# A transformer layer on one core: attention exponentials multiplied by their softmax factor before the transposes, outputs kept transposed for the out-projection

## The chip, the core and the metric

The kernel runs as one program on one core of a Trainium2 chip. The metric is the device time of one execution in microseconds. A core has TensorE (PE in the profile, its weight loads PEld), VectorE (DVE), ScalarE (ACT), GpSimd (POOL) and SyncE (SP), which work side by side and meet at semaphores. PE writes to PSUM; the other engines read it and move results to SBUF.

## The reference, cut to what matters

One decoder layer with 1024 tokens of width 1024, all in float32: a feed-forward half step, token mixing, and a second feed-forward half step. The token mixing is what the change touches:

```python
h = u @ w_in                                  # 1976 columns: queries, keys, values, gate logits, latents
# sparse attention, 8 heads in 2 groups of 4, head width 64; e = exp(s - max s) under the mask, l = sum e
o_nsa = g0 * softmax(q k_cmp) v_cmp + g1 * softmax(q k_sel) v_sel + g2 * softmax(q k_win) v_win
#        63 compressed keys           all causal keys (16 of 16 blocks)  window of 512 keys
# g = sigmoid(gate logits), one per token, head and branch
# latent attention, 8 heads, causal
o_mla = softmax((q_nope k_nope + q_rope k_rope) * scale) v
y = concat([o_nsa, o_mla]) @ w_out
x = layer_norm(ALPHA * x + (1 + gate) * y)
```

## The kernel before, in words

Every product keeps float32 precision by splitting each operand into a high part (rounded for PE) and a low part (the rest), and adding two or three products. So every operand of PE costs ACT one pass (`hi`, a copy) and DVE one pass (`lo`, a subtraction).

The kernel goes stage by stage. Those that matter here: `sparse_inputs` (890 to 924 us in the profile), the sparse attention `nsa` (to 1217), the inputs of the latent attention (to 1273), the latent attention `mla` (to 1449), the turning of the heads' outputs `turn3` (to 1462) and the out-projection `out` (to 1555). All outputs of the input projection lie in one SBUF tile `h` (128 tokens x 8 row tiles x 1976 columns), and the attention writes its results over the queries there.

Both attentions run through `attend` on a list of `Unit`s. A unit is four rows of scores (128 x up to 1024 keys) that share keys: in `nsa` one tile of 128 tokens, one group (four heads) and one branch (0 is causal over i+1 key blocks, 1 the window of up to 5 blocks, 2 the compressed keys, one block of 64), 48 units in all; in `mla` one head and one half of the tokens, 16 units of 4 or 8 key blocks. The steps of a unit:

- **stage**: PE turns the queries, ACT and DVE split them (for `mla` also keys);
- **score**: PE computes scores and adds masks, DVE takes the row maximum (`neg_max`), ACT writes `exps` and its row sums;
- **turn**: for each key block four PE transposes of 128 x 128 exponentials into one of three PSUM banks (`ring`), ACT copies `turned_hi`, DVE subtracts `turned_lo`;
- **apply**: PE multiplies values (64 columns of high parts beside 64 of low parts) with `turned_hi` and then with `turned_lo` into `out_ps`; it has 128 rows (high and low results) and 512 columns (four rows of tokens);
- **finish**: ACT copies `out_ps` to `out_sb` (L2769), PE turns it back with four transposes (L2741), DVE adds high and low halves (`joined`, L2816) after computing the factor one over the row sum (L2809, L2813), and POOL multiplies by factor and gate and adds the branches (L2829 to L2842). In `nsa` POOL also scales the latents in 16 of these steps (`scale_latents`, L2915).

The order on each engine is written out by `plan`, which simulates the steps with prices from a table (`pe_price`, `act_price`, `dve_price`) and takes at each moment the step that can start first. Each engine runs its list strictly in that order. `exps` has 3 rooms in `nsa` and 4 in `mla`, so scores run at most that many units ahead of the turns.

After `mla`, `modulated_transpose` ("turn3") turns the 64 blocks of outputs with PE into `u_hi` and `u_lo`, while SP fetches the first four chunks of `w_out` and the rows `x` to which the result is added. Then `project` ("out") runs: DVE multiplies a chunk of weights by a gate row (L2003), ACT and DVE split it (L1983, L2006), and PE makes 24 matmuls of 128x512 for each of 16 chunks (L2044).

## Time and profile before

| | |
|---|---|
| median of three runs | 2229.32 us (2226.71 to 2231.69) |
| profiled execution | 2232.52 us, of which the span of its instructions is 2230.7 us |
| PE, DVE, ACT, POOL busy, share of the span | 95%, 68%, 45%, 27% |
| `nsa`, 924.4 to 1217 us | 292.6 us; PE busy 275.2, DVE 238.0, ACT 226.4, POOL 78.4 |
| `mla`, 1272.7 to 1450 us | 177.3 us; PE 169.2, DVE 129.1, ACT 117.4, POOL 9.8 |
| `turn3`, 1450 to 1464.8 us | 14.8 us; PE 9.4, DVE 11.6, ACT 9.2 |
| `out`, 1464.8 to 1555 us | 90.2 us; PE 89.1, DVE 29.6, ACT 9.5 |

Busy times are unions: where an instruction starts before the last one has ended, the overlap counts once. The mean of a single instruction is therefore a little longer than the distance to the next.

### The profile page before, as it was taken

Reading aid. Unit: us, or ns where it says so; the run is one execution under the profiler, and the core shown is the slowest. Engines: PE = TensorE matmul, PEld = TensorE weight load, DVE = VectorE, ACT = ScalarE, POOL = GpSimd, SP = SyncE. Lnnn points to the kernel's source line nnn. Section 1 sums busy time; section 2 is a strip of 40 time slices with the busy share of each in tenths; the row PEclk is TensorE's granted clock in tenths of the full one; section 3 lists DMA queues with packets and bytes.
Section 4 is the critical chain, followed back from the end, with each engine's and each line's share of the span. In section 5 each row is a group of like instructions: output and inputs, shape, how many; then the busy total and the mean of one; then the engine's idle time right before and its main releaser. Section 6 shows DMA issues by size and latency. Waiting matters only on the chain. (4 is left out here: it accounts for less than half of the span.)

```text
span 2230.7 us, 29121 instructions
## 1 busy us (share of the span) xinstructions
PE 2115.3 (95%) x10361; PEld 1771.7 (79%) x10361; DVE 1508.7 (68%) x2361; ACT 1001.9 (45%) x1925; POOL 599.0 (27%) x597
## 2 busy tenths in 40 slices
PE   5999999999999999799998899998999999999997
PEld 4888888878887887688886789877788888887885
DVE  6877777766886414687887577744765555558689
ACT  3433333334554112887886467621733323324443
POOL 0366656611100000132312000000245555540301
PEclk9999999999998999799999899989999999999998
DMA  7255544468831310300000000041333333347975
GB/s 268 88 168 170 166 165 162 168 206 267 249 109 56 126 46 18 117 1 1 1 1 1 1 1 1 1 151 36 112 118 113 104 118 109 105 127 259 293 258 100
DMA packets 193638, 254.46 MB, mean 114 GB/s; under 512 B 18192, under 2 KB 116560, under 8 KB 193495
## 3 DMA queue, kind: packets, MB, share of 16 engines
q1 hardware_dynamic: 178088, 208.04, 28.1%
q0 software_dynamic: 15408, 44.57, 7.7%
q8 instruction: 83, 1.36, 0.2%
q14 instruction: 59, 0.48, 0.1%
HBM read 212.72 MB, written 43.52 MB: 115 GB/s over the span
## 5 line engine op out<-in xcount | busy, mean ns | idle before, releaser
L781 DVE TENSOR_TENSOR ffn2A_u<-ffn2A_u,ffn_banks 128x512 f32<-128x512 f32 x60 | 41.2, 687 | 118.5 <-PE ffn_banks L725 112.4
L2757 ACT ACTIVATE nsaa_exps<-nsaa_scores,nsaa_neg_max 128x64 f32<-128x64 f32 (+8 forms) x192 | 108.3, 578 | 23.5 <-DVE nsaa_neg_max L2790 15.1
L2805 DVE TENSOR_TENSOR nsaa_turned_lo<-nsaa_ring,nsaa_turned_hi 128x512 fp32r<-128x512 f32 (+1 forms) x148 | 96.7, 683 | 23.4 <-ACT nsaa_turned_hi L2766 22.2
L1315 DVE SCALAR_TENSOR_TENSOR late_part_late<-ada_rows,far_silu_c,late_part_late 128x1024 f32<-128x1024 f32 x56 | 107.2, 1914 | 3.3 <-DMA ada_rows<-in_w_ada 3.2
L602 ACT ACTIVATE ffn1A_t_hi<-ffn1A_t 128x512 fp32r<-128x512 f32 x80 | 48.5, 628 | 132.2 <-POOL ffn1A_t L595 100.3
L602 ACT ACTIVATE ffn2A_t_hi<-ffn2A_t 128x512 fp32r<-128x512 f32 x80 | 48.4, 628 | 122.1 <-POOL ffn2A_t L595 93.8
L2044 PE MATMUL in_acc<-mix_in_w_hi,mix_in_u_hi 128*128 128x494 f32 x256 | 99.4, 388 | 0.7 <-PEq L85 0.7
L2044 PE MATMUL in_acc<-mix_in_w_lo,mix_in_u_hi 128*128 128x494 f32 x256 | 99.1, 387 | 0.0
L2044 PE MATMUL in_acc<-mix_in_w_hi,mix_in_u_lo 128*128 128x494 f32 x256 | 99.0, 387 | 0.0
L725 PE MATMUL ffn_banks<-ffn1S_s_hi,ffn1A_t_hi 128*128 128x512 f32 x240 | 93.8, 391 | 0.0
L725 PE MATMUL ffn_banks<-ffn1S_s_hi,ffn1A_t_lo 128*128 128x512 f32 x240 | 93.4, 389 | 0.0
L725 PE MATMUL ffn_banks<-ffn2S_s_hi,ffn2A_t_hi 128*128 128x512 f32 x240 | 93.4, 389 | 0.0
L725 PE MATMUL ffn_banks<-ffn1S_s_lo,ffn1A_t_hi 128*128 128x512 f32 x240 | 93.4, 389 | 0.0
L725 PE MATMUL ffn_banks<-ffn2S_s_lo,ffn2A_t_hi 128*128 128x512 f32 x240 | 93.4, 389 | 0.0
L725 PE MATMUL ffn_banks<-ffn2S_s_hi,ffn2A_t_lo 128*128 128x512 f32 x240 | 93.4, 389 | 0.0
L2766 ACT ACTIVATE nsaa_turned_hi<-nsaa_ring 128x512 fp32r<-128x512 f32 (+1 forms) x148 | 83.3, 599 | 20.1 <-PE nsaa_ring L2725 19.3
L2725 PE MATMUL nsaa_ring<-all_ident,nsaa_exps 128*128 128x128 f32 (+1 forms) x592 | 82.9, 275 | 2.7 <-DVE nsaa_turned_lo L2805 2.5
L2006 DVE TENSOR_TENSOR mix_in_w_lo<-mix_in_w_raw,mix_in_w_hi 128x494 fp32r<-128x494 f32 x28 | 18.8, 672 | 97.4 <-ACT mix_in_w_hi L1983 97.4
L619 DVE TENSOR_TENSOR ffn2A_t_lo<-ffn2A_t,ffn2A_t_hi 128x512 fp32r<-128x512 f32 x80 | 73.8, 945 | 13.9 <-ACT ffn2A_t_hi L602 12.9
L781 DVE TENSOR_TENSOR ffn1A_u<-ffn1A_u,ffn_banks 128x512 f32<-128x512 f32 x60 | 41.0, 684 | 58.5 <-PE ffn_banks L725 58.5
L2725 PEld LDWEIGHTS nsaa_ring<-all_ident,nsaa_exps 128*128 128x128 f32 (+1 forms) x592 | 68.1, 138 | 11.0 <-DVE nsaa_turned_lo L2805 4.2
L997 PE MATMUL ffn_banks<-ffn2B_d_hi 128*128 128x512 f32 x188 | 73.6, 392 | 2.5 <-ACT ffn2R_p L1040 1.7
(643 smaller groups left out, 6921.2 us busy)
## 6 DMA issues: line engine op xcount, KB each, us to landing
ada_rows<-in_w_ada POOLq DMA_DIRECT2D x56, 512.0 KB, 4.7
ffn_raw_g<-in_ffn_wg SPq DMA_DIRECT2D x44, 512.0 KB, 3.7
ffn_raw_u<-in_ffn_wu SPq DMA_DIRECT2D x44, 512.0 KB, 4.9
early_w<-in_w_ada SPq DMA_DIRECT2D x16, 512.0 KB, 7.0
mix_in_w_raw<-in_w_in SPq DMA_DIRECT2D x32, 247.0 KB, 2.6
ffn_rest<-in_ffn_wd SPq DMA_DIRECT2D x29, 256.0 KB, 5.0
hidden<-ffn1A_c SPq DMA_DIRECT2D x22, 256.0 KB, 4.5
hidden<-ffn1A_u SPq DMA_DIRECT2D x22, 256.0 KB, 5.0
```

Of the source, the lines that this page charges most:

```text
L602: act.activation(self.b_hi[w][:, :], self.block_of(w), ACT.Copy).then_inc(self.rounded, 1)
L619: dve.tensor_tensor(self.b_lo[w][:, :], self.block_of(w), self.b_hi[w][:, :].bitcast(F32), ALU.subtract).then_inc(self.split, 1)
L725: last = pe.matmul(out, b[w][:, cols], u[a][:, c, :], start=(not joins and c == 0 and m == 0), stop=(c == KC - 1 and m == 2), skip_group_c ...
L781: dve.tensor_tensor(out, base, bank, ALU.add).then_inc(self.mixed, 1)
L997: last = pe.matmul(self.banks[:, 4 * QUAD[p] + i, :], h[:, rows], w[:, HALF:D], start=(j == 0 and at == 0 and not JOINS[p]), stop=(j == PA ...
L1315: dve.scalar_tensor_tensor(out=part_late[:, v, :], in0=ada[:, n % 2, :], scalar=silu_c[:, k:k + 1], in1=part_late[:, v, :], op0=ALU.mult, ...
L2006: dve.tensor_tensor(lo[:, k, :], raw[:, k, :], hi[:, k, :].bitcast(F32), ALU.subtract).then_inc(split, 1)
L2044: last = pe.matmul(acc[:, i, 0:width], u[:, c, i * P:(i + 1) * P], w[:, c % slots, :], start=(c == 0 and m == 0), stop=(c == DC - 1 and m ...
L2725: last = pe.transpose(bank[0:u.keys, r * P:(r + 1) * P], exps[n % slots][:, r, k * u.keys:(k + 1) * u.keys], ident[:, :])
L2757: made = act.activation(u.kept(r, exps[n % slots]), u.seen(r, scores[:, m % 2, :]), ACT.Exp, bias=neg_max[:, n % SUMS, r:r + 1], accum_out ...
L2766: act.activation(turned_hi[0:u.keys, j % copies, cols], bank[0:u.keys, cols], ACT.Copy).then_inc(hi_done, 1)
L2805: dve.tensor_tensor(turned_lo[0:u.keys, j % copies, cols], bank[0:u.keys, cols], turned_hi[0:u.keys, j % copies, cols].bitcast(F32), ALU.s ...
```

## The change

1. **Weighing ahead.** The exponentials are multiplied in place by gate / row sum before they are transposed. The first `by_vector` key blocks are done by DVE, four `tensor_scalar` (one for each row) in a step `weigh`; in `nsa` `by_vector` is (blocks + 1) // 3 for branch 0 and zero for the others, in `mla` it is 0 for a first half and 3 for a second. Each other key block is one POOL `tensor_tensor` of 128x4x128 elements (4x64 for the compressed branch, fewer rows at the diagonal in `mla`). A turn waits for its weighing, no longer for the exponentials.
2. **Factor.** A step `factor` on DVE makes max(sum, 1e-30) * (1 + exp(-gate logit)) in one instruction, and its reciprocal. `gates` holds 1 + exp(-logit), made by ACT with Exp and a DVE addition at the end of `sparse_inputs`. DVE also takes over `scale_latents`.
3. **One PSUM group for three branches.** The three branches of a tile are summed in `out_ps`: `out_ps` opens with branch 0 and closes with branch 2 (16 groups in `nsa`, and 16 in `mla`, one for each unit).
4. **Folding in place of finishing.** At the end of a group ACT copies the half of `out_ps` that lies on the other partitions into `other`, and DVE adds it to the half in place and writes the result to `h`, still transposed. The 4 transposes, the copy, `joined` and the POOL work of each unit go.
5. **Compressed branch.** Values lie twice in `vc` (partitions 0 to 63 and 64 to 127), high and low parts of the turned exponentials one above the other, so that its apply is one matmul.
6. **Rooms.** Each branch of `nsa` has two rooms for its exponentials (six in all), some in columns of `h` that are no longer read; `mla` has four as before.
7. **Out-projection.** `turn3` goes. In `project` ACT copies and DVE subtracts 128x1024 elements of `h` for each chunk of its first block (`u_hi`, `u_lo`), and the loads of weights, gate row and `x` are issued there.

```diff
@@ dve_price, pool_price
+    if kind == "weigh":
+        return 4 * (60 + u.by_vector * u.keys * 0.52)
...
+    return 100 + (4 - u.weighed_rows(k)) * u.keys * 2.9
@@ needs (plan)
+        if kind == "factor":
+            return [("act", last_score[n])]
+        if kind == "weigh":
+            return [("dve", ("factor", n, 0))]
@@ attend, tensor
-                    pe.wait_ge(exped, last_score[n] + 1)
+                    if k < u.by_vector:
+                        pe.wait_ge(weighed_dve, weigh_no["weigh", n, 0] + 1)
+                    else:
+                        pe.wait_ge(weighed_pool, weigh_no["weigh", n, k] + 1)
...
-                    if k == 0 and n:
-                        pe.wait_ge(out_moved, n)
...
+                    if k == 0 and u.opens and u.group:
+                        pe.wait_ge(folded, u.group)
+                    start, stop = u.opens and k == 0, u.closes and k == len(u.blocks) - 1
+                    if u.one_block:
+                        last = pe.matmul(out_ps[:, :], u.value_of(0), turned_hi[:, j % copies, :], start=start, stop=stop)
...
-                else:
-                    pe.wait_ge(out_moved, n + 1)
-                    for r in range(4):
-                        last = pe.transpose(bank[:, r * P:(r + 1) * P], out_sb[:, r, :], ident[:, :])
@@ attend, vector
+                elif kind == "factor":
+                    b = n % SUMS
+                    dve.wait_ge(exped, last_score[n] + 1)
...
+                        dve.scalar_tensor_tensor(out=floor[:, b, :], in0=sums[:, b, :], scalar=1e-30, in1=u.gate,
+                                                 op0=ALU.max, op1=ALU.mult).then_inc(floored, 1)
+                    if beside is not None:
+                        beside(dve, n)
+                    dve.wait_ge(floored, n + 1)
                     dve.reciprocal(factor[:, b, :], floor[:, b, :]).then_inc(factored, 1)
...
+                elif kind == "weigh":
+                    dve.wait_ge(factored, n + 1)
+                    for r in range(4):
+                        at = u.room[:, r, 0:min(u.widths[r], u.by_vector * u.keys)]
+                        last = dve.tensor_scalar(at, at, factor[:, n % SUMS, r:r + 1], None, ALU.mult)
+                    last.then_inc(weighed_dve, 1)
+                elif kind == "fold":
+                    dve.wait_ge(moved, u.group + 1)
+                    folding.dve(dve, u.group, out_ps, other).then_inc(folded, 1)
@@ attend, gpsimd
+                pool.wait_ge(factored, n + 1)
+                top = u.weighed_rows(k)
+                at = u.room[:, top:4, k * u.keys:(k + 1) * u.keys]
+                by = factor[:, n % SUMS, top:4].unsqueeze(2).to_broadcast([P, 4 - top, u.keys])
+                pool.tensor_tensor(at, at, by, ALU.mult).then_inc(weighed_pool, 1)
@@ project
+            if reload is not None:
+                chunks.ahead(sp)
             load(0, slots)
+            if reload is not None:
+                for i in range(TT):
+                    sp.dma_start(out[:, i, :], reload[i * P:(i + 1) * P, :]).then_inc(out_in[0], 16)
...
+                if u_raw is not None and n == 0:
+                    act.activation(u_hi[:, c, :].rearrange("p (i q) -> p i q", q=P), u_raw[c], ACT.Copy).then_inc(u_hi_done, 1)
...
+                if u_raw is not None and n == 0:
+                    dve.wait_ge(u_hi_done, c + 1)
+                    dve.tensor_tensor(u_lo[:, c, :].rearrange("p (i q) -> p i q", q=P), u_raw[c],
+                                      u_hi[:, c, :].bitcast(F32).rearrange("p (i q) -> p i q", q=P), ALU.subtract).then_inc(u_split, 1)
```

How the lists change, at three places. First DVE in `nsa`, in the tiles with five or more key blocks, around the factor of a branch-0 unit. Before (`floor`, `factor` and `joined` are the finish):

```order
L2809 TENSOR_SCALAR nsaa_floor<-nsaa_sums 128x4
L2813 RECIPROCAL nsaa_factor<-nsaa_floor 128x4
L2816 TENSOR_REDUCE nsaa_joined<-nsaa_ring 128x256
L2805 TENSOR_TENSOR nsaa_turned_lo<-nsaa_ring,nsaa_turned_hi 128x512
L2786 TENSOR_REDUCE nsaa_neg_max<-nsaa_scores 128x1 x2
```

Now:

```order
L2831 SCALAR_TENSOR_TENSOR nsaa_floor<-nsaa_sums,masks_gates 128x4
L2836 RECIPROCAL nsaa_factor<-nsaa_floor 128x4
L2823 TENSOR_TENSOR nsaa_turned_lo<-nsaa_ring,nsaa_turned_hi 128x512
L2841 TENSOR_SCALAR h_h<-h_h,nsaa_factor 128x256 x4
L2823 TENSOR_TENSOR nsaa_turned_hi<-nsaa_ring,nsaa_turned_hi 64x512
```

Four instructions on the exponentials (here in a room in `h`) stand one subtraction behind the reciprocal, ahead of the next subtractions and maxima.

POOL in `nsa`, its first rows there. Before:

```order
L2829 TENSOR_TENSOR nsaa_factor_g<-nsaa_factor,masks_gates 128x4
L2842 TENSOR_TENSOR h_h<-nsaa_joined,nsaa_factor_g 128x256
L2915 TENSOR_SCALAR h_h<-h_h,sparse_rstd 128x384
L2829 TENSOR_TENSOR nsaa_factor_g<-nsaa_factor,masks_gates 128x4
L2837 TENSOR_TENSOR nsaa_joined<-nsaa_joined,nsaa_factor_g 128x256
L2840 TENSOR_TENSOR h_h<-h_h,nsaa_joined 128x256
```

Now (a branch 0 and a branch 1 run together where the tile's rooms have one name):

```order
L2856 TENSOR_TENSOR nsa_exps<-nsa_exps,nsaa_factor 128x4x128 x5
L2856 TENSOR_TENSOR nsa_exps<-nsa_exps,nsaa_factor 128x256
L2856 TENSOR_TENSOR h_h<-h_h,nsaa_factor 128x4x128 x7
L2856 TENSOR_TENSOR nsa_exps<-nsa_exps,nsaa_factor 128x256
L2856 TENSOR_TENSOR nsa_exps<-nsa_exps,nsaa_factor 128x4x128 x8
```

POOL now has a run of large multiplications for each unit, released by the same reciprocal as DVE's four.

PE from the end of `mla` into the out-projection. Before:

```order
L2735 MATMUL mlaa_out_ps<-mlaa_turned_lo,latent_v 128x128
L2741 MATMUL mlaa_ring<-all_ident,mlaa_out_sb 128x128 x4
L85 UNCONDITIONAL_BRANCH
L203 UNCONDITIONAL_BRANCH
L145 MATMUL turn_tp<-all_ident,h_h 128x128 x64
L85 UNCONDITIONAL_BRANCH
L2035 UNCONDITIONAL_BRANCH
L2044 MATMUL out_acc<-out_w_hi,mix_out_u_hi 128x512
```

Now:

```order
L2757 MATMUL mlaa_out_ps<-mlaa_turned_hi,latent_v 128x128
L2758 MATMUL mlaa_out_ps<-mlaa_turned_lo,latent_v 128x128
L86 UNCONDITIONAL_BRANCH
L2015 UNCONDITIONAL_BRANCH
L2026 MATMUL out_acc<-out_w_hi,mix_out_u_hi 128x512
```

The last 4 transposes of `mla` and the 64 of `turn3` are gone, and the first matmul of the out-projection is the next that PE does.

## Rows read from the trace of the kernel before

**Rows 1.** The page's first part: busy time, share of the span, instructions.
```profile
PE 2115.3 (95%) x10361; PEld 1771.7 (79%) x10361; DVE 1508.7 (68%) x2361; ACT 1001.9 (45%) x1925; POOL 599.0 (27%) x597
```

**Rows 2.** Table by stretch: from:to, us, busy (instructions) per engine, clock, DMA.
```profile
924.40:1217.00 292.60, 275.23 (x1784) 234.91 (x1784) 237.96 (x444) 226.40 (x613) 78.36 (x143) 0.98 0.03 9
...
1272.70:1450.00 177.30, 169.21 (x1066) 150.54 (x1067) 129.10 (x244) 117.35 (x276) 9.81 (x16) 0.97 0.00 1
1450.00:1464.80 14.80, 9.40 (x65) 9.15 (x63) 11.58 (x19) 9.16 (x17) 0.00 (x0) 0.73 0.93 354
1464.80:1555.00 90.20, 89.09 (x384) 73.35 (x384) 29.58 (x48) 9.48 (x15) 0.00 (x0) 0.98 0.13 42
```

**Rows 3.** Groups of instructions in `nsa`: busy us, mean ns, idle before, releaser.
```profile
L2816 DVE TENSOR_REDUCE nsaa_joined<-nsaa_ring 128x256 f32<-128x512 f32 x48 | 32.0, 666 | 5.0 <-PE nsaa_ring L2741 5.0
...
L2741 PE MATMUL nsaa_ring<-all_ident,nsaa_out_sb 128*128 128x128 f32 x192 | 29.3, 275 | 2.6 <-ACT nsaa_out_sb L2769 1.6 <-DVE nsaa_joined L2816 0.5 <-DVE nsa_q L2879 0.4
...
L2837 POOL TENSOR_TENSOR nsaa_joined<-nsaa_joined,nsaa_factor_g 128x256 f32<-128x256 f32 x32 | 19.6, 613 | 14.2 <-DVE nsaa_joined L2816 14.2
...
L2879 DVE SCALAR_TENSOR_TENSOR nsa_q<-nsaa_ring,nsa_q 64x256 fp32r<-64x256 f32 x32 | 13.5, 422 | 6.3 <-ACT nsa_q L2874 5.8
...
L2735 PE MATMUL nsaa_out_ps<-nsaa_turned_lo,sparse_vc 64*128 64x512 f32 x16 | 6.3, 393 | 0.0
```

**Rows 4.** The same view of `mla`.
```profile
L2741 PE MATMUL mlaa_ring<-all_ident,mlaa_out_sb 128*128 128x128 f32 x64 | 9.6, 273 | 0.8 <-ACT mlaa_out_sb L2769 0.8
```

**Rows 5.** Timeline near the end of `mla`: start, us, engine, line.
```profile
1444.66 0.46 PEld L2741 LDWEIGHTS mlaa_ring<-all_ident,mlaa_out_sb 128*128 128x128 f32 x4
...
1445.09 0.19 PEld L2735 LDWEIGHTS mlaa_out_ps<-mlaa_turned_hi,latent_v 128*128 128x128 f32 x1
```

**Rows 6.** Groups on DVE over the whole run.
```profile
L667 DVE CAST ffn1S_a_hi<-plain_u 128x512 fp32r<-128x512 f32 x8 | 3.4, 421 | 1.6 <-ACT plain_u L641 1.6
...
L974 DVE TENSOR_TENSOR ffn2B_d_lo<-ffn_rest,ffn2B_d_hi 128x1024 fp32r<-128x1024 f32 x9 | 11.0, 1219 | 0.0
```

**Rows 7.** Timeline in `nsa`, POOL and DVE side by side.
```profile
991.30 1.25 POOL L2915 TENSOR_SCALAR h_h<-h_h,sparse_rstd 128x384 f32<-128x384 f32 x1
...
992.06 0.51 DVE L2809 TENSOR_SCALAR nsaa_floor<-nsaa_sums 128x4 f32<-128x4 f32 x1
992.60 0.18 DVE L2813 RECIPROCAL nsaa_factor<-nsaa_floor 128x4 f32<-128x4 f32 x1
```

**Rows 8.** The line L2809: durations ns min/median/max, first and last start.
```profile
L2809 DVE TENSOR_SCALAR nsaa_floor<-nsaa_sums x48: 148/160/507, 943.9 to 1214.5; 128x4 f32<-128x4 f32 x48
```

**Rows 9.** Timeline in the second feed-forward stage, POOL and DVE side by side.
```profile
1610.89 1.75 POOL L595 TENSOR_TENSOR ffn2A_t<-ffn_raw_u 128x512 f32<-128x512 f32 x1
...
1611.41 1.78 DVE L671 TENSOR_TENSOR ffn2S_s_lo<-plain_u,ffn2S_s_hi 128x512 fp32r<-128x512 f32 x1
...
1612.72 1.61 POOL L595 TENSOR_TENSOR ffn2A_t<-ffn_raw_g,ffn2A_t 128x512 f32<-128x512 f32 x1
1613.11 1.77 DVE L692 TENSOR_TENSOR plain_u<-plain_u 128x512 f32<-128x512 f32 x1
1614.81 0.68 DVE L671 TENSOR_TENSOR ffn2S_s_lo<-plain_u,ffn2S_s_hi 128x512 fp32r<-128x512 f32 x1
```

**Rows 10.** Timeline of `turn3` and the start of the out-projection.
```profile
1447.82 0.61 POOL L2842 TENSOR_TENSOR h_h<-h_h,mlaa_factor 128x256 f32<-128x256 f32 x1 [0.97 <-DVE h_h L2816]
1449.52 0.34 SPq L1890 DMA_DIRECT2D w_out_gate<-gate_rows  x1
...
1462.65 0.69 DVE L2003 TENSOR_TENSOR w_out_w_raw<-w_out_w_raw,w_out_gate 128x512 f32<-128x512 f32 x1 [0.40 <-PEq L85]
...
1464.78 0.80 PE L2044 MATMUL out_acc<-out_w_hi,mix_out_u_hi 128*128 128x512 f32 x1 [5.40 <-DVE out_w_lo L2006]
```

**Rows 11.** DMA issues: KB each, median us from issue to landing.
```profile
w_out_w_raw<-in_w_out SPq DMA_DIRECT2D x16, 256.0 KB, 2.7
mix_out_x<-x_rows SPq DMA_DIRECT2D x8, 512.0 KB, 9.2
```

More of the change, by code:

```diff
@@ L1892, in ahead, with project @@
             self.load(sp, 0, c)
-def project(nc, stage, chunks, blocks, u_hi, u_lo, out, out_in=None, beside=None):
+def project(nc, stage, chunks, blocks, u_hi, u_lo, out, out_in=None, beside=None, u_raw=None, reload=None):
     slots, width, gated_too = chunks.SLOTS, chunks.width, chunks.gate_dram is not None
@@ L2039, in one @@
                     pe.wait_ge(split, n * DC + c + 1)
+                    if u_raw is not None and n == 0:
+                        pe.wait_ge(u_split, c + 1)
                     for i in range(TT):
@@ L2429, with __init__ @@
 class Unit:
-    def __init__(self, blocks, keys, first_row, key_of, widths, mask_of, value_of, out, adds, gate, before, terms, stage_price):
+    def __init__(self, blocks, keys, first_row, key_of, widths, mask_of, value_of, group, opens, closes, gate, before, terms,
+                 stage_price, by_vector, room):
         self.blocks = blocks
@@ L2439, in __init__ @@
         self.value_of = value_of
-        self.out = out
-        self.adds = adds
+        self.group, self.opens, self.closes = group, opens, closes
         self.gate = gate
@@ L2543, in plan @@
         applying += [("apply", n, k) for k in range(len(u.blocks))]
-        finishing += [("finish", n, 0)]
+        factors += [("factor", n, 0)]
+        for k0, k1 in u.parts_weighed():
+            (by_vector if k0 < u.by_vector else by_pool).append(("weigh", n, k0))
+        if u.closes:
+            folding += [("fold", n, 0)]
     scores = [x for x in scoring if x[0] == "score"]
@@ L2564, in needs @@
                 return [("dve", x)]
+            if kind == "fold":
+                return [("pe", ("apply", n, len(u.blocks) - 1))]
             if kind == "turn" and turn_no[x] >= copies:
@@ L2568, in needs @@
         if engine == "dve":
[L2569 removed]
+            return [("pe" if kind == "score" else "act", x)]
         found = []
[L2571 removed]
+        if kind in ("turn", "stage") and len(ring) >= BANKS:
             found.append(("dve", ring[len(ring) - BANKS]))
@@ L2914, in scale_latents, with halves, act, dve @@
                 at = h[:, i, col:col + rank]
-                pool.tensor_scalar(at, at, rstd[:, which, i:i + 1], None, ALU.mult)
-        tiles = list(range(2, TT)) + [0, 1]
+                dve.tensor_scalar(at, at, rstd[:, which, i:i + 1], None, ALU.mult)
+        class Folding:
+            def halves(self, group, out_ps):
+                rows = out_ps[:, :].rearrange("p (c odd q) -> p c odd q", c=2, odd=2)
+                for odd in range(2):
+                    own, far = slice(odd * HD, (odd + 1) * HD), slice((1 - odd) * HD, (2 - odd) * HD)
+                    yield own, rows[own, :, odd, :], rows[far, :, odd, :]
+            def act(self, act, group, out_ps, other):
+                for own, here, there in self.halves(group, out_ps):
+                    last = act.activation(other[own, 0:2 * P].rearrange("p (c q) -> p c q", c=2), there, ACT.Copy)
+                return last
+            def dve(self, dve, group, out_ps, other):
+                g, i = group // TT, tiles[group % TT]
+                for own, here, there in self.halves(group, out_ps):
+                    at = h[own, i, COL_Q + g * HPG * HD:COL_Q + (g + 1) * HPG * HD].rearrange("p (c q) -> p c q", c=2)
+                    last = dve.tensor_tensor(at, here, other[own, 0:2 * P].rearrange("p (c q) -> p c q", c=2), ALU.add)
+                return last
@@ new lines, in sparse_attention @@
+        tiles = list(range(2, TT)) + [0, 1]
+        vacant = {0: [s.sb("exps0", [P, 4, T]), h[:, 0:4, COL_KC:COL_KC + 6 * P]],
+                  1: [s.sb("exps1", [P, 4, 5 * P]), h[:, 4:8, COL_KC:COL_KC + 5 * P]],
+                  2: [s.sb(f"exps2{m}", [P, 4, CMP_PAD]) for m in range(2)]}
+        rooms = {}
+        for g in range(GROUPS):
+            for i in tiles:
+                for b in range(3):
+                    n = 1 if b == 0 and i >= 6 and vacant[0][0].shape[2] < T else 0
+                    rooms[b, i, g] = vacant[b].pop(n)
+                    vacant[b].append(rooms[b, i, g])
@@ L2976, in unit @@
             b = head % 2
-            col = COL_QM + head * HD
-            out = h[:, 4 * half:4 * half + 4, col:col + HD]
             def key_of(r, c0, w):
```

247 lines of the change are left out of this document (108 added, 139 removed).

## The prediction

> **What bounds the kernel now.** I read the page's totals first [rows 1]: PE is busy 95% of the span, DVE 68%, POOL 27%. A share over the whole run says little about one stage, so next comes the table by stretch [rows 2]. In `nsa` PE works 275.2 of 292.6 us and DVE 238.0, in `mla` 169.2 and 129.1 of 177.3. PE sets both lengths, and DVE is not far behind in `nsa` (81%). `turn3` is 14.8 us, then 5.4 of its last microseconds are a wait of PE [rows 10]. So the change, which takes work from PE, gains only if nothing else comes up to meet it. POOL, at 78.4 us in `nsa`, is to become a large worker there.
>
> **PE's part.** The finish of a unit has four transposes. Their group lists 29.3 us in `nsa` for 48 units, 0.61 us each, and 9.6 us in `mla` for 16 [rows 3, 4]; but matmuls overlap, and the weight loads show that the next work is let in 0.43 us after the first of four (1444.66 to 1445.09) [rows 5]. I take 0.43: 20.6 us in `nsa`, 6.9 in `mla`; the group's own sums are the upper ends. The second apply of the compressed branch goes 16 times: 6.3 us by its row [rows 3] as the upper end, and by overlap, as above, some 4 (taken). PE in `nsa` falls to about 251, in `mla` to 162.
>
> **DVE's part, alone.** In `nsa` 48 `joined` of 0.666 go, 32.0 us [rows 3]. Folding adds 16 times two 64x256 operations. None of this kind is in the trace; the nearest, with a PSUM and an SBUF operand and this shape, took 0.422 [rows 3]: 13.5 us. Weighing adds 14 units (seven tiles in two groups) x 4 instructions of 128, 256 or 384 columns. The nearest SBUF-to-SBUF operation with one tensor in is a cast of 512 columns in 0.421 [rows 6]; with 0.16 for the shortest [rows 8], a column costs about 0.5 ns, so 0.22 to 0.36 us each and 56 x 0.27 = 15 us. The 16 scalings of latents (384 or 256 columns) are 5 us likewise. Sum: 238.0 - 32.0 + 13.5 + 15 + 5 = 240 us. In `mla`: 16 `joined` less (10.7 at the same 0.67), 16 folds of 512 columns (0.68, as a 128x512 operation took in [rows 9]) 10.9, 8 x 4 weighings at 0.36 11.4: 129.1 + 11.6 = 141 us. ACT loses: 48 copies of 512 columns against 32 of 256. It bounds nothing.
>
> **POOL's part.** One multiplication with a broadcast factor took 0.613 for 256 columns [rows 3]; 512 columns should be 1.23. Each group has 54 of these (66 key blocks less 12 of DVE) and 8 small ones: 2 x (54 x 1.23 + 8 x 0.61) = 143 us, half of the stage. As a sum that is no bound. In `mla` it is 8 x 24 row blocks x 0.31 = 59 us.
>
> **What the two do to each other.** This is the term on which the forecast rests. In [rows 7] POOL works from 991.30 to 992.55, and DVE's `floor`, four elements wide and 0.16 as a rule, begins at 992.06 and lasts 0.51: it ends just behind POOL. The longest of 48 is 0.507 at a median of 0.160 [rows 8]. The reciprocal behind it isn't touched (0.18). With work queued on both sides they alternate [rows 9]: POOL from 1610.89 to 1612.64, DVE's operation stands until 1613.19 (1.78 instead of 0.68), POOL's next from 1612.72 to 1614.33, DVE's next again 1.77; once POOL is done, 0.68. So one DVE operation from SBUF to SBUF that meets POOL waits for the rest of one POOL operation, and the next waits for a whole one.
>
> Now DVE's four weighings stand one subtraction (0.68) behind the reciprocal that also releases POOL's run for the same unit. The first waits for half of a POOL operation, 0.6, the others 1.23 each, as long as POOL has parts: for tiles of 2 to 8 blocks POOL has 1, 2, 3, 3, 4, 5, 5, so 21 of a group's 28 meet one. That is 7 x 0.6 + 14 x 1.23 = 21.4 us a group, 43 in `nsa`. Of the 48 `floor`, which now read two SBUF operands, and of 16 scalings of latents about half meet POOL at 0.6 to 1.2: 21. Together 64 us (bounds: 0, if the four run through unhindered; 98, if all 56 and all 64 meet POOL: 14 x 0.6 + 42 x 1.23 + 64 x 0.6). In `mla` a second half has POOL parts of 1.23, 1.23, 0.92, 0.61: 0.6 + 1.23 + 0.92 + 0.61 = 3.4, eight times 27, and 3 for `floor`: 30 us (0 to 34).
>
> The Trainium skill has the rule for this, in "SBUF — State Buffer", section "Who interferes with whom": VectorE's two-port modes (`tensor_scalar` can enter them) and two-SBUF-input operations share a port pair with GpSimd under an exclusive lock, and the one that comes second is fully blocked; a reduction never is. The trace agrees where it can, with 0.51 instead of 0.16. No row shows a `tensor_scalar` with a factor for each partition under it: by the rule all of them pay, by the median floor none would.
>
> **`nsa` then.** DVE 240 + 64 = 304 us, more than PE's 251, so DVE is the bound. It can't be busy all the time: at least a few us at head and tail, at most the 17.4 that PE, the present bound, stands. I take 6: 310 us, +17.4. The planner knows no such wait (the price in its table for the four is 0.5 to 1.0 us), so `turned_lo` and maxima queued behind come late and PE stands at its turns.
>
> **`mla`.** DVE 141 + 30 = 171, with 6 at the ends 177; PE 162 + 8 = 170. So 177, no change. Bounds: 169 (PE alone) and 184.
>
> **Out-projection.** `mla` ends 1.3 us earlier: 4 transposes, `joined` and POOL (until 1448.43) [rows 10] give way to a fold. The first DMA went out at 1449.52; say 1448.2 now. Gate row and first chunk land after 2.7 (a chunk's median) to 9.2 us (when `x` was fetched at once; now it queues behind) [rows 11]; I take 4.4. Then gate 0.69, `u_lo` of 1024 columns 1.22 [rows 6], `w_lo` 0.69 and some 0.2 between: PE starts at 1455.4 instead of 1464.78, -9 (bounds -11 and -5). The later seven chunks' `u` work (ACT 1, DVE 1.2 us) is hidden: DVE has 2.6 us for each, and PE takes 90.2 / 16 = 5.6. No POOL runs there.
>
> **`sparse_inputs`.** One more copy and subtraction of `vc` and one addition on `gates`: +0.5. The table that Exp needs now loads there in place of Sigmoid's, and not again in `nsa`, where DVE and PE covered it: 0.
>
> **Sum.** 17.4 + 0 - 9 + 0.5 = +9 on the profiled execution's 2232.5, 2241.5. That execution lies 3.2 above the median, so 2238 against 2229.3. Its own range is 2222 to 2250, by DVE waits of 50 to 75 us in `nsa`.
>
> **Rivals.** (A) *No collision*: the weighings run through, or POOL is idle then; PE stays the bound. For it: the median floor is short [rows 8], and POOL would still stand for half of the stage. Against: the four are released with POOL's run. `nsa` 251 + 17.4 less the 2.6 that PE stood before the removed transposes [rows 3], 266 (-26.8); `mla` -8; -9; +0.5: -43, 2186. It decides once waits stay under some 15 us in `nsa`. (B) *Half*: DVE's waits fall into time in which it would have stood anyway (54.6 us idle now), or number half. `nsa` 240 + 32 + 10 = 282 (-10.6), `mla` 170 (-7): -26, 2203. (C) *Full, and passed on*: DVE reaches only the 94% that PE has today, since its list is fixed and waits for PE in between. `nsa` 304 / 0.94 = 323, `mla` 171 / 0.94 = 182: +30 + 5 - 9 + 0.5, 2256.
>
> **Chances.** Forecast 0.45, A 0.20, B 0.17, C 0.18. About 0.2% (4.5 us) is what a measurement can tell from no change. Of the forecast's 0.45, 0.03 lies below it, 0.12 within and 0.30 above. So faster 0.40, same 0.12, slower 0.48. The range leaves out some 0.1 of A's low side and 0.05 of C's high side, where all 98 us of waits would count: 2184 to 2266.
>
> **What would show it.** In the changed profile: the weighing `tensor_scalar` on DVE at a mean near 1.2 us (A: 0.3); `floor` at a mean near 0.4 us; DVE over 95% of `nsa` at 310 us (A: PE at 94% of 265); PE's waits there on `turned_lo` or the weighed exponentials above 40 us in sum; the first out-projection matmul 7 us after the stage's first DMA. I am wrong if weighings are short, or if they are long and PE still sets the stage.

## The result, and the profile after

The changed kernel takes **2275.03 us** (median of 4 runs, 2270.59 to 2278.93) against 2230.18 us for the kernel before beside it (4 runs, 2226.71 to 2231.69): a ratio of 1.020, 95% interval 1.018 to 1.022. It is slower by 2%. The forecast was 2238.0, with a range of 2184 to 2266. The sign of the likeliest case was right and the size was not (+9 forecast, +45 measured): the time lies 9 us above the range.

The page's totals of the changed kernel, against [rows 1]:

```profile
span 2277.1 us, 28320 instructions
...
PE 2105.3 (92%) x10025; PEld 1754.8 (77%) x10025; DVE 1583.9 (70%) x2443; ACT 993.3 (44%) x1901; POOL 685.6 (30%) x633
```

PE does 336 instructions less and is busy for 10 us less, in a span that is 46 us longer. The table by stretch says where, against [rows 2] (from:to, us, busy and instructions of PE, PEld, DVE, ACT, POOL, granted clock, DMA share, GB/s; `nsa`, `mla`, the wait for the out-projection, the out-projection):

```profile
926.00:1237.80 311.80, 265.41 (x1577) 224.74 (x1578) 278.35 (x500) 215.37 (x597) 120.58 (x124) 0.93 0.02 8
...
1293.10:1500.72 207.62, 178.94 (x1000) 153.91 (x1000) 161.70 (x276) 120.24 (x276) 55.71 (x72) 0.90 0.00 1
1500.72:1508.60 7.88, 0.00 (x0) 0.00 (x0) 2.46 (x4) 2.63 (x3) 0.00 (x0) 0.52 0.64 200
1508.60:1598.40 89.80, 89.78 (x383) 74.09 (x384) 36.24 (x52) 15.19 (x21) 0.00 (x0) 0.97 0.22 82
```

Cut at the same marks (a stage from its first matmul to the next stage's, `mla` to the first DMA behind it), the kernel before had 294.0 in `nsa`, 176.8 in `mla` and 15.3 of wait. So `nsa` is 18 us longer (forecast 17.4), `mla` 31 us (forecast 0), the wait 7 us shorter (forecast 9 for the out-projection); some 5 us are scattered over the rest. Two numbers in these rows go against the forecast or were not in it: DVE is busy for only 89% of `nsa` (over 95% was expected) and 78% of `mla`, and the granted clock is 0.93 and 0.90, where it was 0.98 and 0.97 [rows 2].

The weighing on DVE, the term on which the forecast rested, in three rows (line, engine, operation, count: durations in ns, minimum/median/maximum), and the row for `floor`, which was 148/160/507 in [rows 8]:

```profile
L2841 DVE TENSOR_SCALAR nsa_exps<-nsa_exps,nsaa_factor x40: 273/953/1194, 937.6 to 1225.3; 128x128 f32<-128x128 f32 x16, 128x256 f32<-128x256 f32 x16, 128x384 f32<-128x384 f32 x8
L2841 DVE TENSOR_SCALAR mla_exps<-mla_exps,mlaa_factor x32: 762/1084/1300, 1320.4 to 1489.4; 128x384 f32<-128x384 f32 x32
L2841 DVE TENSOR_SCALAR h_h<-h_h,nsaa_factor x16: 274/924/1127, 952.3 to 1126.2; 128x128 f32<-128x128 f32 x8, 128x256 f32<-128x256 f32 x8
```

```profile
L2831 DVE SCALAR_TENSOR_TENSOR nsaa_floor<-nsaa_sums,masks_gates 128x4 f32<-128x4 f32 x48 | 13.9, 290 | 2.7 <-ACT nsa_exps L2774 1.9 <-ACT h_h L2774 0.6
```

None of the 32 in `mla` took less than 762 ns, where 0.36 us had been put for one alone. What this does to PE shows in the timeline of a second half in `mla` (start, us, engine, line):

```profile
1440.33 0.17 DVE L2829 TENSOR_SCALAR mlaa_floor<-mlaa_sums 128x4 f32<-128x4 f32 x1
1440.53 0.18 DVE L2836 RECIPROCAL mlaa_factor<-mlaa_floor 128x4 f32<-128x4 f32 x1
1440.74 4.00 DVE L2841 TENSOR_SCALAR mla_exps<-mla_exps,mlaa_factor 128x384 f32<-128x384 f32 x4
1440.79 4.21 POOL L2856 TENSOR_TENSOR mla_exps<-mla_exps,mlaa_factor 128x512 f32<-128x512 f32 x5 [12.79 <-DVE mlaa_factor L2836]
...
1442.13 0.40 PE L2728 MATMUL mlaa_scores<-mla_k_hi,mla_q_lo 96*128 96x512 f32 x1
1444.66 0.67 DVE L3013 TENSOR_TENSOR mla_k_lo<-mlaa_ring,mla_k_hi 64x512 fp32r<-64x512 f32 x1
...
1444.88 1.88 PE L2744 MATMUL mlaa_ring<-all_ident,mla_exps 128*128 128x128 f32 x12 [2.36 <-DVE mla_exps L2841]
1445.55 1.85 ACT L2783 ACTIVATE mlaa_turned_hi<-mlaa_ring 128x512 fp32r<-128x512 f32 x3 [3.35 <-PE mlaa_ring L2744]
...
1449.08 0.78 PE L2757 MATMUL mlaa_out_ps<-mlaa_turned_hi,latent_v 128*128 128x512 f32 x1
```

DVE's four and POOL's five start 0.05 us apart, on the same reciprocal. The four last 4.00 us. PE runs out of other work at 1442.5 and stands for 2.36 us, since its next instruction turns a block that DVE weighs. Then a matmul of 512 columns takes 0.78 us at 1449.08, where most take 0.39, and the granted clock is lower for a part of the next 6 us (the table by stretch around that place, columns as above):

```profile
1440.00:1442.50 2.50, 2.50 (x15) 1.88 (x13) 2.40 (x5) 2.01 (x8) 1.71 (x2) 1.00 0.03 7
1442.50:1444.88 2.38, 0.03 (x1) 0.03 (x1) 2.38 (x4) 0.00 (x0) 2.38 (x4) 1.00 0.00 0
1444.88:1448.00 3.12, 3.12 (x18) 2.83 (x19) 3.12 (x6) 2.33 (x6) 0.11 (x1) 0.74 0.00 0
1448.00:1451.00 3.00, 3.00 (x17) 2.72 (x17) 1.94 (x6) 1.63 (x4) 1.85 (x3) 0.70 0.00 0
1451.00:1455.00 4.00, 4.00 (x26) 3.50 (x25) 3.16 (x6) 2.31 (x7) 0.91 (x2) 1.00 0.00 0
```

With one of its two levels, 1.2 GHz, for a part of these two stretches, PE did about 0.26 x 3.12 + 0.30 x 3.00 = 1.7 us of work less than at 2.4 GHz. So a standstill of 2.4 us costs about 4. The same place of another unit, cut more finely (the standstill, and the lower clock behind it):

```profile
1347.01:1349.37 2.36, 0.00 (x1) 0.03 (x1) 2.36 (x4) 0.00 (x0) 2.36 (x4) 1.00 0.00 0
1349.37:1350.80 1.43, 1.42 (x11) 1.14 (x12) 1.43 (x3) 0.76 (x2) 0.12 (x1) 1.00 0.00 0
1350.80:1354.20 3.40, 3.40 (x16) 3.28 (x14) 2.76 (x7) 2.37 (x7) 0.52 (x1) 0.50 0.00 0
1354.20:1358.00 3.80, 3.80 (x24) 3.25 (x23) 2.91 (x5) 2.56 (x6) 2.23 (x4) 1.00 0.02 4
```

The waits of PE in `mla` (engine, line, waited for: us, times, longest) show that it happens at each of the eight second halves:

```profile
PE mlaa_ring L2744 <- DVE mla_exps L2841: 21.7, 8, 5.3
```

### The profile page after: what moved, and what is told of

Read it like the earlier page. It is cut to its first block and busy times, and to the rows that moved or that the text cites. A ratio compares the mean times of both kernels' runs of the same rounds, so it can differ in the third digit from the quotient of the medians.

```text
span 2277.1 us, 28320 instructions
## 1 busy us (share of the span) xinstructions
PE 2105.3 (92%) x10025; PEld 1754.8 (77%) x10025; DVE 1583.9 (70%) x2443; ACT 993.3 (44%) x1901; POOL 685.6 (30%) x633
## 5 line engine op out<-in xcount | busy, mean ns | idle before, releaser
L2856 POOL TENSOR_TENSOR nsa_exps<-nsa_exps,nsaa_factor 128x512 f32<-128x512 f32 (+1 forms) x78 | 74.0, 973 | 136.4 <-DVE nsaa_factor L2836 136.4
L2823 DVE TENSOR_TENSOR nsaa_turned_lo<-nsaa_ring,nsaa_turned_hi 128x512 fp32r<-128x512 f32 x132 | 86.9, 681 | 8.3 <-ACT nsaa_turned_hi L2783 6.5
L2774 ACT ACTIVATE nsa_exps<-nsaa_scores,nsaa_neg_max 128x64 f32<-128x64 f32 (+8 forms) x136 | 71.8, 539 | 26.2 <-DVE nsaa_neg_max L2807 17.2
L2744 PE MATMUL nsaa_ring<-all_ident,nsa_exps 128*128 128x128 f32 (+1 forms) x384 | 60.0, 288 | 19.6 <-DVE nsa_exps L2841 14.0
```

The source lines that it names most:

```text
L2744: last = pe.transpose(bank[0:u.keys, r * P:(r + 1) * P], u.room[:, r, k * u.keys:(k + 1) * u.keys], ident[:, :])
L2774: made = act.activation(u.kept(r, u.room), u.seen(r, scores[:, m % 2, :]), ACT.Exp, bias=neg_max[:, n % SUMS, r:r + 1], accum_out=sums[:, ...
L2823: dve.tensor_tensor(low, bank[0:u.keys, cols], turned_hi[0:u.keys, j % copies, cols].bitcast(F32), ALU.subtract).then_inc(ring_free, 1)
L2856: pool.tensor_tensor(at, at, by, ALU.mult).then_inc(weighed_pool, 1)
```

## Experiments

The theory after the comparison, **collision**: DVE's weighings are short by themselves and become long because POOL weighs at the same time; PE's list stands behind them. Two rivals. **The longer way**: any weighing between the last exponential and the first transpose makes PE stand, long or short. **The fixed order**: PE's list was made for short weighings, and another list would hide long ones. Stage lengths of all runs, cut at the same marks in each run's one profiled execution; the totals are medians, and the ratios are to runs of the kernel before made beside each (2229.4 to 2232.2 us). Executions of one kernel differ by 2 to 10 us in total, so a stage's difference of 1 or 2 us says little.

| kernel | `nsa` us | `mla` us | total us (median) | ratio to before, 95% |
|---|---|---|---|---|
| before | 294.0 | 176.8 | 2230.18 | |
| changed | 311.8 | 207.6 | 2275.03 | 1.018 to 1.022 |
| pool_none | 268.8 | 177.9 | 2203.37 | 0.985 to 0.991 |
| dve_none | 279.6 | 173.7 | 2209.28 | 0.988 to 0.993 |
| both_none | 269.0 | 175.1 | 2195.88 | 0.982 to 0.988 |
| dve_tiny | 304.3 | 198.9 | 2260.69 | 1.010 to 1.016 |
| price | 309.4 | 206.6 | 2274.07 | 1.017 to 1.022 |
| act_weighs | 274.7 | 189.1 | 2221.06 | 0.993 to 0.997 |
| both_pool | 281.0 | 185.3 | 2222.57 | 0.994 to 0.997 |
| mla_all_dve | 314.2 | 185.8 | 2254.46 | 1.008 to 1.012 |
| pool_behind | 283.4 | 177.9 | 2214.00 | 0.990 to 0.994 |
| combo | 273.9 | 180.2 | 2211.23 | 0.988 to 0.993 |
| pool_halves | 288.0 | 189.3 | 2233.65 | 1.000 to 1.002 |
| combo2 | 273.2 | 177.9 | 2207.40 | 0.988 to 0.991 |

### POOL's weighings left out

```
-            for step in order["pool"]:
+            for step in []:
...
-                        pe.wait_ge(weighed_pool, weigh_no["weigh", n, k] + 1)
+                        pe.wait_ge(factored, n + 1)
```

> The changed kernel with POOL's weighings left out (those blocks go to their transposes unweighed, as soon as the reciprocal is there); DVE's four weighings stay, and every engine's order. Collision theory: DVE's weighing shares nothing with POOL any more and takes 0.3 us in the mean (1.06 in mla before), floor 0.16; PE stands at weighed exponentials under 6 us in mla; mla 207.6 to about 178, nsa 311.7 to about 285; total about 2219. Rival, the longer way (last exponential, floor, reciprocal, weighing, first transpose, with a fixed order on PE): weighings are short and PE still stands: mla over 198, nsa over 300, total over 2253.

Measured: `nsa` 268.8, `mla` 177.9. The weighing of 384 columns is 410/415/421 ns, no outlier among 32:

```profile
L2841 DVE TENSOR_SCALAR mla_exps<-mla_exps,mlaa_factor x32: 410/415/421, 1274.2 to 1412.5; 128x384 f32<-128x384 f32 x32
```

`floor` is at 158 ns in the mean. POOL's work beside DVE and PE is worth 43 us in `nsa` and 30 in `mla`, more than the whole loss. That run takes away all of POOL's effects at once; that it is the meeting on DVE, and not POOL being late, is what the runs below separate. The longer way fails as a cause of the loss: the weighing is still ahead of the transposes, and PE waits for it 2.8 us in `mla` (one place of the eight), not 21.7. The total, 2203.37, is 16 us below my number (2219), all of it in `nsa`.

### DVE's weighings left out

```
-                    for r in range(4):
-                        at = u.room[:, r, 0:min(u.widths[r], u.by_vector * u.keys)]
-                        last = dve.tensor_scalar(at, at, factor[:, n % SUMS, r:r + 1], None, ALU.mult)
-                    last.then_inc(weighed_dve, 1)
...
-                        pe.wait_ge(weighed_dve, weigh_no["weigh", n, 0] + 1)
+                        pe.wait_ge(factored, n + 1)
```

> The changed kernel with DVE's weighings left out (their blocks go to the transposes unweighed, on the reciprocal's signal); POOL's stay, and every engine's order. Collision theory: what DVE's four cost goes, 32 us of DVE in mla and 41 in nsa, and with it PE's wait; floor stays at a mean near 0.29 us; mla about 180, nsa about 290, total about 2226. Rival, the longer way: the four are only the last step of it, PE still stands at the reciprocal: mla over 195, total over 2253. Rival, POOL is late: PE then stands at POOL's parts, total over 2253 too, with POOL as the releaser.

Measured: 279.6 and 173.7, total 2209.28, each below my number (290, 180, 2226). POOL isn't late (no wait of PE for it in `mla`, 0.5 us in `nsa`). Beside the next run, 10.6 us of `nsa` are left that come with POOL's work. `floor` is at 276 ns instead of 158 and the latents' scalings are at 520 to 669 instead of 345 to 412: DVE's other SBUF-to-SBUF work is stretched too. That these two make up the 10.6 us is not shown: 4.6 of them are idle time of PE and 6.0 are busy time of the same matmuls, at a granted clock of 0.95 instead of 0.96.

### No weighing at all

The edits of both runs above together.

> The changed kernel without any weighing, on DVE or POOL; all else and every order the same. What is left is what the removed transposes, the fold and the missing transposes ahead of the out-projection are worth by themselves. Collision theory: nsa about 270, mla about 170, total about 2196. Rival, the longer way: nsa over 285, mla over 190, total over 2232.

Measured: 269.0 and 175.1, total 2195.88. This is what the removed transposes and the fold are worth: 25 us in `nsa` and 1.7 in `mla`. The first agrees with rival A (26.8), the second does not (8; before this run I had put `mla` at 170): see below.

### DVE's weighings cut to four columns

```
-                        at = u.room[:, r, 0:min(u.widths[r], u.by_vector * u.keys)]
+                        at = u.room[:, r, 0:4]
```

> The changed kernel with DVE's four weighings cut to 4 columns each (the other columns of these blocks stay unweighed); POOL's stay whole. Tells whether DVE pays for POOL by instruction or by element. By instruction (a wait for a POOL operation's rest, or for a whole one): the four take 0.6 to 0.9 us in the mean though alone they would take 0.16, mla about 198, total about 2258. By element (the two share a path in turn): the four take under 0.3 us, and the run is as the one without them, about 2226.

```profile
L2841 DVE TENSOR_SCALAR mla_exps<-mla_exps,mlaa_factor x32: 654/976/1109, 1311.8 to 1472.3; 128x4 f32<-128x4 f32 x32
```

An instruction with a hundredth of the elements takes 976 ns instead of 1084. The price is by instruction, not by element. `mla` (198.9, expected 198) and the total (2260.69, expected 2258) are as expected for it.

### POOL's weighings cut in two

```
-                top = u.weighed_rows(k)
-                at = u.room[:, top:4, k * u.keys:(k + 1) * u.keys]
...
-                pool.tensor_tensor(at, at, by, ALU.mult).then_inc(weighed_pool, 1)
+                for top, end in ((u.weighed_rows(k), 2), (max(2, u.weighed_rows(k)), 4)):
+                    if top < end:
+                        at = u.room[:, top:end, k * u.keys:(k + 1) * u.keys]
...
+                        last = pool.tensor_tensor(at, at, by, ALU.mult)
+                last.then_inc(weighed_pool, 1)
```

> The changed kernel with each of POOL's weighings cut into two of half the rows (128x256 at 0.61 us instead of 128x512 at 1.04); DVE's, all waits and every order as in the changed kernel. Nothing is left out. Theory 'a DVE instruction waits for one POOL instruction': the four weighings in mla fall from 1.06 to about 0.61 us in the mean, nsa's of 256 columns from 0.97 to about 0.6; mla about 190, nsa about 300, total about 2246. Theory 'DVE stands as long as POOL has work at all', or shares by the element: POOL's time for the unit is even longer, so the four stay at 1.0 us or more; mla 207 or more, total 2275 or more.

```profile
L2841 DVE TENSOR_SCALAR mla_exps<-mla_exps,mlaa_factor x32: 762/764/874, 1296.3 to 1447.5; 128x384 f32<-128x384 f32 x32
```

POOL does more work (139 us in `nsa` instead of 121) and the kernel is 41 us faster, 2233.65, with `nsa` at 288.0 and `mla` at 189.3 (expected 2246, 300 and 190). A DVE instruction waits for about one POOL instruction: with POOL's at 0.61 us it takes 0.76, with POOL's at 1.04 it takes 1.08. It was expected at 0.61; some of its own 0.41 shows.

PE's standstills in `mla` are shorter here: at six of the eight places 1.15 to 1.3 us where they were 2.2 to 2.4, and behind those six the granted clock stayed at 1.00. One of them, and the time behind it:

```profile
1406.60:1407.89 1.29, 0.00 (x0) 0.03 (x1) 1.29 (x3) 0.00 (x0) 1.29 (x3) 1.00 0.00 0
1407.89:1411.50 3.61, 3.61 (x25) 3.02 (x26) 3.61 (x7) 2.94 (x8) 1.61 (x4) 1.00 0.00 0
```

The Trainium skill, "SBUF — State Buffer", section "Who interferes with whom", has a rule that fits this run and the one before: the shared port pair is an exclusive lock held for a whole instruction, and the one that comes second is fully blocked. The two rows agree. It also says that the order of issue decides who is blocked; in the trace of the changed kernel POOL's side lost little: its five took 4.21 us beside DVE's four, and 3.75 in a run in which they start behind them (POOL behind DVE, below).

### Another price in the planner

```
-        return 4 * (60 + u.by_vector * u.keys * 0.52)
+        return 4 * 1050
```

> The changed kernel with one number of the planner changed: DVE's four weighings are priced at 4 x 1.05 us, as measured under POOL, in place of 0.9 us. The work is the same, the order of PE, DVE and ACT differs. Theory 'fixed order' (the stretch hurts because PE's list was made for short weighings): PE gets other work ahead of these turns, its wait for weighed exponentials in mla falls from 21.7 to under 8 us, mla from 207.6 to about 192, nsa from 311.8 to about 303, total about 2251. Theory 'DVE's own time' (whatever the order, the stretched weighings push subtractions and maxima back): mla over 202, nsa over 308, total over 2265.

Measured: 2274.07, `nsa` 309.4, `mla` 206.6, PE's wait in `mla` 21.7 as before. In `mla` the planner made almost the same list (at one place two transposes stand ahead of a pair of matmuls and not behind it), so there the run tests nothing but that this planner has nothing else to put in. In `nsa` the lists differ at many places, and it gained 2 us. So knowing the stretched price didn't help this planner; whether another list could hide the stretch was not tried.

### ACT weighs instead of DVE

```
-                        last = dve.tensor_scalar(at, at, factor[:, n % SUMS, r:r + 1], None, ALU.mult)
+                        last = act.activation(at, at, ACT.Copy, scale=factor[:, n % SUMS, r:r + 1])
```

(and the step moved from DVE's list to ACT's, with a price of its own there)

> DVE's four weighings go to ACT (a copy with the factor as scale, same blocks, same columns); POOL's stay. Nothing is left out. Collision theory: ACT shares nothing with POOL, four of them take 0.3 to 0.6 us each, only floor and the scaling of latents on DVE stay stretched (the run without DVE's weighings had 279.6 us in nsa and 173.7 in mla): nsa about 281, mla about 176, total about 2212. Rival, the longer way: what matters is how late the first blocks are weighed, and ACT's list is late for it (it also makes turned_hi): nsa over 297, mla over 190, total over 2243.

Measured: 2221.06, faster than before by 0.5%. `nsa` 274.7, better than expected (281); `mla` 189.1, 13 us above my number (176) and beside the rival's (over 190). ACT's four take 0.62 us each in `mla`, but PE waits for them only once (1.5 us). It waits instead for `mla_q_lo`, 6.5 us, and for other subtractions, in a list that the planner made anew. So the rival's size came out in `mla`, but not by its mechanism.

### POOL weighs all

```
-                        (len(blocks) + 1) // 3 if branch == 0 else 0, rooms[branch, i, g])
+                        0, rooms[branch, i, g])
...
-                        None, before, 3, 1360, 3 * half, rooms[2 * b + half])
+                        None, before, 3, 1360, 0, rooms[2 * b + half])
```

> All blocks are weighed by POOL, none by DVE, in both stages. Nothing is left out. Collision theory: DVE's list is free of weighings, floor and latents stay stretched; POOL needs 1.05 us for a block where PE needs some 1.3 to turn and apply one, so only the first is waited for: nsa about 286, mla about 179, total about 2220. Rival, POOL is late (this would be the reason to give a third of the blocks to DVE): PE waits for POOL's parts by over 20 us in sum in mla and over 20 in nsa, total over 2255.

Measured: 2222.57 (7 runs), `nsa` 281.0 (expected 286), `mla` 185.3 (expected 179). PE waits for no POOL part in `mla`. The simplest version, with the whole load on the slower engine, beats the shared one by 52 us and the kernel before by 0.4%.

### DVE weighs all in `mla`

```
-                        None, before, 3, 1360, 3 * half, rooms[2 * b + half])
+                        None, before, 3, 1360, 4 * half + 4, rooms[2 * b + half])
...
-        return 4 * (60 + u.by_vector * u.keys * 0.52)
+        return sum(210 + min(w, u.by_vector * u.keys) * 0.54 for w in u.widths)
```

> In mla all blocks are weighed by DVE, four instructions of whole rows for each unit, so that POOL does nothing there; nsa as in the changed kernel, but for the planner's price of DVE's weighing, now 0.21 us + 0.54 ns a column as measured without POOL. Nothing is left out. Collision theory: DVE's work in mla is more (130 + some 33 = 163 us) but the time is less, since no instruction is stretched: weighings at 0.21 us + 0.54 ns a column, mla about 180, total about 2247. Rival, DVE's load and the later first block bind: mla over 197, total over 2264.

Measured: 2254.46, `mla` 185.8 (expected 2247 and 180). `nsa`, where only the planner's price differs, is 2 us longer than in the changed kernel (314.2). DVE now weighs 640 to 1024 columns in each of the four instructions of a second half, where it weighed 384, and each is shorter than any of the 32 with 384 columns was beside POOL; `mla` is 22 us shorter:

```profile
L2841 DVE TENSOR_SCALAR mla_exps<-mla_exps,mlaa_factor x32: 552/648/751, 1319.5 to 1466.5; 128x640 f32<-128x640 f32 x8, 128x768 f32<-128x768 f32 x8, 128x896 f32<-128x896 f32 x8, 128x1024 f32<-128x1024 f32 x8
```

### POOL behind DVE

```
-                pool.wait_ge(factored, n + 1)
+                if u.by_vector:
+                    pool.wait_ge(weighed_dve, weigh_no["weigh", n, 0] + 1)
+                else:
+                    pool.wait_ge(factored, n + 1)
```

> The changed kernel with one wait moved: POOL's weighings of a unit wait for DVE's four of the same unit, where they waited for the reciprocal, so the two don't start together. Order of every engine, work and result are as in the changed kernel; nothing is left out. Collision theory: in mla, where POOL has nothing left of the unit before, the four take 0.415 us each as in the run without POOL, POOL starts 1.7 us later and is still ahead of PE: mla about 178 (207.6 in the changed kernel). In nsa POOL may still be at another unit's parts, so a part of the stretch stays: mean of 256 columns 0.5 to 0.7 us, nsa about 292. Total about 2226. Rival, POOL's later start is passed on to PE (it stands at POOL's first part by 1.5 us for each of 8 and 14 units): mla over 188, nsa over 300, total over 2245.

Measured: **2214.00** (expected 2226), one wait moved, every list as in the changed kernel. It takes back 61 us and is 0.8% faster than the kernel before. The same place as in the timeline above:

```profile
1388.45 1.41 DVE L2841 TENSOR_SCALAR mla_exps<-mla_exps,mlaa_factor 128x384 f32<-128x384 f32 x4
1389.78 0.67 DVE L3016 TENSOR_TENSOR mla_k_lo<-mlaa_ring,mla_k_hi 64x512 fp32r<-64x512 f32 x1
1389.94 3.75 POOL L2859 TENSOR_TENSOR mla_exps<-mla_exps,mlaa_factor 128x512 f32<-128x512 f32 x5 [12.93 <-DVE mla_exps L2841]
1390.08 1.69 PE L2744 MATMUL mlaa_ring<-all_ident,mla_exps 128*128 128x128 f32 x12
```

The four take 1.41 us instead of 4.00, POOL starts 1.7 us after the reciprocal, and PE doesn't wait at this place. `mla` is 177.9, to the tenth what it was without any POOL. In `nsa` 14.6 us are left beside pool_none (283.4 against 268.8): there the DVE weighings are clean too (median 345 ns of 40; 0.5 to 0.7 us had been expected), but `floor` is still at 290 ns and the latents at 627 to 670.

### Both remedies, and two edits more

combo: ACT's weighings in `nsa`, POOL behind DVE in `mla` (the planner knows of it). combo2: also the latents' scaling on ACT, and the planner's list of `mla` as in the changed kernel.

```
-                dve.tensor_scalar(at, at, rstd[:, which, i:i + 1], None, ALU.mult)
+                act.activation(at, at, ACT.Copy, scale=rstd[:, which, i:i + 1])
```

> ACT makes the first weighings in nsa (as in the run with ACT, 274.7 us there), DVE those in mla with POOL behind it (as in the run sent with this one, but planned so). Nothing is left out. Collision theory: nsa 275, mla about 178, total about 2211, faster than the kernel before by 0.9%. Rival, in mla the order that the planner makes of it matters more than the collision (the versions free of it came out at 185 to 189): mla about 187, total about 2220.

> The version with ACT's weighings in nsa and POOL behind DVE in mla, with two edits more: the 16 scalings of latents, stretched on DVE to 0.52 to 0.67 us, go to ACT, and the planner's order of mla is that of the changed kernel (177.9 us there with POOL behind). Nothing is left out. If what is left of the stretch still costs time: nsa 273.9 to about 270, mla 180.2 to 178, total about 2205. Rival, DVE is no longer near the bound, so its 9 us are worth nothing, or ACT's longer list costs them: nsa 274 or more, total about 2210 to 2216.

Measured: 2211.23 (expected 2211) and **2207.40** (expected 2205), the fastest version with nothing left out: 1.0% faster than the kernel before, 3% faster than the changed one. Of the 4 us between the two, 2.3 are in `mla`, where only the order differs, and 0.7 in `nsa` (expected: 4), so the latents' scaling was worth next to nothing once DVE had room. The order that the planner makes matters as well: with the changed kernel's lists in `mla` and the collision gone the stage takes 177.9 us (pool_none, pool_behind, combo2), with lists made anew it takes 180.2 to 189.1 (combo, both_pool, mla_all_dve, act_weighs). How much of that is the list and how much the engine that weighs is not separated.

## Why the prediction was wrong

- **PE's part: right in `nsa`, wrong in `mla`.** PE was to fall to 251 us in `nsa`; without collision it is at 248. In `mla` it was to fall from 169 to 162, and without any weighing it is at 166.4, with the stage only 1.7 us shorter. A part of this is the clock: the 208 transposes that read exponentials outside `h` had 273 ns in the mean and have 285, but their median is 273 in both; 15 of them ran at the lower clock, and the stage had 0.96 granted where the kernel before had 0.97. In dve_none, at 0.98, PE is busy for 164.3 us and the stage is 3.1 us shorter. So some 4.5 of the 7 us came back at most; why the 64 removed transposes were worth less than 0.43 us for four is open.
- **DVE's part, alone: right.** 240 and 141 us forecast, 237.9 and 140.5 in pool_none. A weighing was put at 0.22 to 0.36 us and is 0.28 (128 columns), 0.35 (256) and 0.415 (384).
- **The collision: the mechanism right, the size too high.** DVE's busy time rose by 40.5 us in `nsa` (forecast 64) and by 21.2 in `mla` (forecast 30). The single instruction was put at 1.23, from POOL at 0.613 for 256 columns doubled; POOL takes 1.04 for 512, and the same factor brings POOL's busy time in `nsa` from the 143 us forecast to 120.6. The sum also put the wait on top of DVE's own time (in `mla` 0.84 + 0.36 = 1.2 us each); the four take 1.06 in the mean.
- **The failed step: "DVE is the bound", stage = DVE's busy time + 6 us.** With the true DVE time it gives 278.4 + 6 = 284 in `nsa` and 161.7 + 6 = 168 in `mla`; measured are 312 and 208. Of the 36 us between the change forecast (+9) and the change measured (+45), 31 lie in `mla`. DVE never was the bound. PE is one list in fixed order, and at one place in each unit it must have the weighed blocks: there the stretch goes over to PE but for what PE still has to do, however idle DVE is otherwise. In `mla` the stretch is 2.6 us a unit (4.00 against 1.41), 21 us in eight; PE's wait for weighed blocks rose by 18.9 (21.7 against 2.8 in pool_none). That `nsa` was forecast at 310 us and came out at 311.8 is luck: two errors cancel, a stretch that was too large and a stage that wasn't DVE's.
- **What the sum lacked: PE's clock.** `mla` in the changed kernel has 18.7 us more of idle PE than in pool_none (207.62 - 178.94 against 177.93 - 167.99) and 10.9 us more of busy PE with the same 1000 matmuls, at a granted clock of 0.90 instead of 0.96. The 29.7 us between the two are these. In `nsa` the 43 us are 25 of idle PE and 18 of busy PE with the same matmuls, at 0.93 instead of 0.97. The prediction has no term for this. That the standstills bring the clock down rests on the order of events in the traces and was not tried by itself: each of the eight here (2.2 to 5.3 us) began at a clock of 1.00, which fell to 0.50 during it or within 1.6 us of its end. In pool_halves six last 1.15 to 1.3 us and the clock stayed at 1.00; in both_none one of 1.3 us was followed by 0.50.
- **The rivals.** Rival C had the mechanism ("passed on to PE, since its list is fixed"), and too little of it: it took DVE at 94%, which [rows 2] show for PE in a stage that PE bounds; DVE's is 78 to 89%. It gave `mla` 182 and a total of 2256, 19 us short. Its probability should have been the largest, and the price that of the place and not of the engine's total: what PE still has ahead of the turn (1.8 us in the timeline, from the reciprocal to 1442.5) against what the four take (4).
- **Out-projection: right.** From the last `mla` matmul's start to the first of the out-projection 1445.3 to 1464.78 before, 1497.99 to 1508.62 after: 8.9 us less, forecast 9. The first chunk landed 5.0 us after its issue, where I took 4.4:

```profile
1501.11 7.82 SPq L1854 DMA_DIRECT2D w_out_w_raw<-in_w_out  x5
1506.14 0.69 DVE L1979 TENSOR_TENSOR w_out_w_raw<-w_out_w_raw,w_out_gate 128x512 f32<-128x512 f32 x1 [6.53 <-DMA w_out_w_raw<-in_w_out]
...
1508.62 0.80 PE L2026 MATMUL out_acc<-out_w_hi,mix_out_u_hi 128*128 128x512 f32 x1 [10.37 <-DVE out_w_lo L1986]
```

- **`sparse_inputs`**: +0.5 forecast; `nsa` starts 1.5 us later, but in the variants, which share everything up to there, its start lies between 922.8 and 928.8 us, so this says nothing for or against the term.

Of the 25 us of idle PE in `nsa` the larger part is waits for DVE's weighings: 14.0 us for those outside `h` and 4.9 for those in `h`, where pool_none has 0.8. The first stand in this group of PE (busy, mean | idle before, by releaser), its 320 transposes of exponentials outside `h`:

```profile
L2744 PE MATMUL nsaa_ring<-all_ident,nsa_exps 128*128 128x128 f32 x320 | 50.6, 291 | 19.6 <-DVE nsa_exps L2841 14.0 <-DVE nsaa_turned_lo L2823 4.6 <-POOL nsa_exps L2856 0.5
```

## What to carry to other kernels

Price a stretched operation at the place where the bounding engine stands behind it, not by adding it to its own engine's busy time: an engine that is idle a fifth of the stage can still set its length. Before a job is shared between VectorE and GpSimd, see whether the two halves are released by the same event; here, ordering one behind the other, giving all to GpSimd, and (in `mla` alone) giving all to VectorE were each faster than both at once. If they must overlap, shorter GpSimd instructions cost less here (2233.65 us against 2275.03), although they kept GpSimd busy for longer.
